# A ring of four places for read-back blocks, and two more slots between the read and the split of x, in a two-model transformer block kernel

## The chip, the cores and the metric

The kernel runs on one core of a Trainium2 chip. The metric is the device time of one execution in microseconds (us). In the profile PE is the engine that multiplies matrices, PEld its weight loads, DVE the vector engine, ACT the scalar engine, POOL the GpSimd engine, and SP the engine that here only issues DMAs.

## The reference

Two transformer blocks run one after the other on x of 256 tokens by 2048 features, all in float32. Cut to what matters here:

```python
# first block
h = rms_norm(x, norm1_g);      proj = h @ w_in              # 2048 -> 6160 columns
mix = concat([gated_linear_attention(...), dilated_attention(...)])
x = x + mix @ w_out                                         # end of stage 1
h2 = rms_norm(x, norm2_g)
x = x + (silu(h2 @ w_gate) * (h2 @ w_up)) @ w_down          # hidden 5632, end of stage 2
# second block, layer 0 (retention and convolution) and layer 1 (window attention)
x = x + even_mixer(rms_norm(x, ev_norm_w), ev_w_in, conv_w, ev_w_out)   # end of stage 3
x = x + odd_mixer(rms_norm(x, od_norm_w), od_w_in, sinks, od_w_out)
```

So a weight matrix is read once, and multiplied with 256 tokens. At three places the finished x becomes the left operand of the next weight matrix: after `w_out` (it is called X1 then), after `w_down` (X2), and after `ev_w_out` (X3).

## The kernel before, in words

**Blocks and units.** The products are cut into 96 blocks of mostly 512 output columns, and these into units of two k tiles (2 x 128 rows of the weights, 512 columns, 512 KB). Each unit is loaded into one of four places of `raw`, copied by ACT to the rounded high part `wh` (L1330) and turned by DVE into the rest `wl = raw - wh` (L1583). PE then runs three products for each k tile and each half of the tokens: `wh` by the high part of x, `wl` by the high part of x, `wh` by the low part of x (L1147 to L1149). That is 12 matmuls of 512 columns in a unit. `wh` and `wl` have three places (`NS = 3`), so ACT begins unit u once PE is through unit u - 3.

**The turned x.** PE needs x with features on partitions, in a high part `xh` (written by ACT) and a low part `xl` (written by DVE). At the end of a stage x comes out token by token in four pieces of 512 columns. Each piece is two pairs of k tiles. The last piece is turned by PE (`xturn`: L1081, then `xh<-m` and `xl<-m`). The pairs of the three pieces before are turned by way of memory: DVE transposes 32 x 32 blocks (`turn`, L1669, 2 instructions), SP writes them to the DRAM tensor `blocks` in four DMAs of 64 KB (`send`, L2154), SP reads them back in another order in one DMA of 256 KB (`fetch`, L2161), and then ACT writes `xh<-A` (2 instructions) and DVE writes `xl<-A` (4 instructions). The last two together are the step `xsent`. The same way (`msent`) is gone by the heads of the mixers.

**The norm.** `norm` is a chain of 13 small instructions on DVE (L1592 the first), which needs the sums of squares that ACT makes (`sq`, L1397, 4 instructions for each piece). Its result scales the outputs, not the operand; PE doesn't wait for it.

**The order.** A planner (`Plan`) writes one list of steps. Each engine takes its own instructions out of this list in the list's order, so the position in the list is the position in every queue. The planner goes on by slots of half a unit. A step that is due later is a generator that gives the number of slots to wait; `fetched` waits 4 slots after the send, says `fetch`, waits 4 more and says `xsent`. It also waits until the step two turns before is through, as the read-back places were two. The loads of the weights stand in SP's queue at the `cut` of unit u, for unit u + 4, and wait until `wl` of unit u is written.

**What a unit waits for.** PE's first matmul of a unit waits for `wl` of that unit (`s_lo`) and for the `xl` of its two k tiles (`s_sent` where they came by way of memory). In the first block of a stage's successor the k tiles 8 and 9 stand in the fifth unit, 10 and 11 in the sixth. In what follows "the fifth unit" and "the sixth unit" are those.

Of the kernel before, what the change touches and what calls it, by code (L numbers as in the profile page):

```python
# [33 lines left out]
class Block:  # L34


    def __init__(self, i, w, row, col, n, kts, acts, done):
        self.i, self.w, self.row, self.col, self.n, self.kts, self.acts, self.done = i, w, row, col, n, kts, acts, done
        self.units = []
# [110 lines left out]
class Plan:  # L150
# [8 lines left out]
    def __init__(self, blocks, units):  # L159
        self.order, self.said, self.there, self.norms, self.emptied = [], set(), {}, 0, set()  # L160
        self.lanes = {"first": [], "att": [], "fin": [], "post": []}
        self.pause = dict.fromkeys(self.lanes, 0)
        self.now, self.through, self.end = 0.0, {"act": 0.0, "dve": 0.0}, {}
        self.turns, self.own = [], 0
        self.blocks, self.units = blocks, units
        self.lay()

# [248 lines left out]
    def turned_and_sent(self, *p):  # L416

        if p[0] == "xsent":
            yield from self.room("dve", .8)
        self.say("turn", *p)  # L420
        self.say("send", *p)
        self.turns.append(p)
        self.spawn(self.fetched(len(self.turns) - 1, p))

    def fetched(self, n, p):
        yield 4
        while n >= 2 and self.turns[n - 2] not in self.said:
            yield 1
        self.say("fetch", *p)
        yield 4  # L430
        self.say(*p)

    def moved_by_blocks(self, key, j):
# [178 lines left out]
def program(nc, t, out):  # L612
# [7 lines left out]
    plan = Plan(blocks, units)  # L620
# [37 lines left out]
    opened = {p: n + 1 for n, p in enumerate(opens)}  # L658
# [18 lines left out]
    sents = {p: n + 1 for n, p in enumerate(q for q in plan.order if q[0] in ("xsent", "msent"))}  # L677
# [11 lines left out]
    with ctx:  # L689
        def sb(name, shape, dt=f32):  # L690
            return ctx.enter_context(nc.sbuf_tensor(name, shape, dt))

        def sem(name):
            return ctx.enter_context(nc.semaphore(name))
# [10 lines left out]
        A1 = sb("A1", [128, 6144])  # L705
        A2 = sb("A2", [128, 6144])
# [9 lines left out]
        memory = t["blocks"].rearrange("(n p) c -> n p c", n=4)  # L716
# [14 lines left out]
        s_pv, s_ob_act, s_ob_dve = sem("s_pv"), sem("s_ob_act"), sem("s_ob_dve")  # L731
        s_split = sem("s_split")
        s_turn, s_sent = sem("s_turn"), sem("s_sent")
        s_send, s_fetch = [sem("s_send0"), sem("s_send1")], [sem("s_fetch0"), sem("s_fetch1")]
        s_sq, s_nsum = sem("s_sq"), sem("s_nsum")
        s_root = sem("s_root")
        s_act_step, s_dve_step, s_pool_step = sem("s_act_step"), sem("s_dve_step"), sem("s_pool_step")
# [4 lines left out]
        s_g_sq, s_g_sum, s_g_n = sem("s_g_sq"), sem("s_g_sum"), sem("s_g_n")  # L742
# [178 lines left out]
        def raw_free(u):  # L921

            return s_lo, max((v + 1 for v in range(u) if raw_lane(v) % NR == raw_lane(u)), default=0)
# [27 lines left out]

        def turn_places(p):

            n = (sents[p] - 1) % 2
            if p[0] == "msent" and p[3] == "r":
                return PB[:, :, 256:384], A2[:, 5128:5640].rearrange("p (i n) -> p i n", i=4)
            at = {"d": A2[:, 4096:6144], "o": A2[:, 2560:4608], "X1": A2[:, 0:2048],
                  "X2": A2[:, 0:2048], "X3": A1[:, 0:2048]}[p[3] if p[0] == "msent" else p[1]]
            a, b = at[:, 512 * n:512 * n + 512], at[:, 1024 + 512 * n:1536 + 512 * n]
            return (z.rearrange("p (i n) -> p i n", i=4) for z in (a, b))  # L960

        def read_back(p, i):
# [7 lines left out]
        def sent(p):  # L970

            n = sents[p] - 1
            return s_send[n % 2], 64 * (n // 2 + 1)

        def back(p):

            n = sents[p] - 1
            return s_fetch[n % 2], 16 * (n // 2 + 1)

        def last_sent(*start):  # L980
            return [p for p in sents if p[:len(start)] == start][-1]
# [1 line left out]
        def turn_place_free(p):  # L983

            kind = p[3] if p[0] == "msent" else p[1]
            if kind == "d":
                return [(s_move, moves[("move", "qk", "k", 1, 3)])]
            if kind == "X1":
                return [(s_pv, opened[("g_o", 3)])]
            if kind == "r":  # L990
                return [(s_g_n, 4), (s_pv, opened[("apv", "d", 7)]), (s_sent, sents[p] - 1)]
            if kind == "X3":
                return [(s_pv, opened[("r_pv", 3)])]
            if kind == "o":
                return [(s_move, moves[("move", "cg", 0, 1, 3)]), (s_cmix, 4)]
            return []
# [1103 lines left out]
        def sync(e):  # L2100
            on = Once(e)

            def load(u):
                if u >= SINGLE:
                    on.wait_ge(*raw_free(u))
                weights(e, u)

            def turned_x(i):
                k0, k1 = XPARTS[i]
                e.dma_start(xT[:, k0:k1, :], t["xT"].rearrange("p (k t) -> p k t", k=KT)[:, k0:k1, :]  # L2110
                            ).then_inc(s_xt[i], 16)

            n0, n1 = COLS["n1"]
            turned_x(0)
            e.dma_start(small[:, n0:n1], t["small"][:, n0:n1]).then_inc(s_n1, 16)
            turned_x(1)
            load(2)
            turned_x(2)
            load(3)
            load(4)  # L2120
            turned_x(3)
            load(5)
            load(6)
            turned_x(4)
            load(7)
            turned_x(5)
            for p in plan.order:
                kind, a = p[0], p[1:]
                if kind == "cut" and a[0] + NR >= SINGLE and a[0] + NR < N:
                    u = a[0] + NR  # L2130
                    load(u)
                    if u == 8:
                        turned_x(6)
                    if u in (9, 11, 13, 15):
                        j = (u - 9) // 2
                        e.dma_start(x[:, :, 512 * j:512 * j + 512], t["x"].rearrange("(t p) d -> p t d", p=128)
                                    [:, :, 512 * j:512 * j + 512]).then_inc(s_x[j], 16)
                    elif u == 16:
                        e.dma_start(rel, t["rel"]).then_inc(s_rel, 16)
                        e.dma_start(oh, t["oh"]).then_inc(s_rel, 16)  # L2140
                        e.dma_start(lnn, t["lnn"]).then_inc(s_rel, 16)
                        for i in range(2):
                            e.dma_start(w2[16 * i:16 * i + 16, :], t["w2"]).then_inc(s_w2, 16)
                        e.dma_start(small[:, 0:n0], t["small"][:, 0:n0]).then_inc(s_small, 16)
                    elif u == 17:
                        e.dma_start(small[:, n1:], t["small"][:, n1:]).then_inc(s_small, 16)
                elif kind == "send":
                    n = sents[a] - 1
                    on.wait_ge(s_turn, n + 1)
                    if n >= 4:  # L2150
                        on.wait_ge(*back(plan.turns[n - 4]))
                    blocks_, _ = turn_places(a)
                    for i in range(4):
                        e.dma_start(memory[n % 4].rearrange("(b p) (i n) -> i p b n", b=4, i=4)[i],  # L2154
                                    blocks_[32 * i:32 * i + 32]).then_inc(s_send[n % 2], 16)
                elif kind == "fetch":
                    n, (_, to) = sents[a] - 1, turn_places(a)
                    on.wait_ge(*sent(a))
                    if n >= 2:
                        on.wait_ge(s_sent, n - 1)  # L2160
                    e.dma_start(to, memory[n % 4].rearrange("p (i n) -> p i n", i=4)).then_inc(s_fetch[n % 2], 16)  # L2161
                elif kind == "out":
                    j = a[0]
                    if j == 3:
                        on.wait_ge(s_added, 1)
                        e.dma_start(out[0:128, 1536:2048], x[:, 0, 1536:2048]).then_inc(s_out, 16)
                        on.wait_ge(*x_ready(4, 3))
                        e.dma_start(out[128:256, 1792:2048], x[:, 1, 1792:2048]).then_inc(s_out, 16)
                        continue
                    on.wait_ge(*x_ready(4, j))  # L2170
                    for k in range(2):
                        e.dma_start(out[128 * k:128 * k + 128, 512 * j:512 * j + 512],
                                    x[:, k, 512 * j:512 * j + 512]).then_inc(s_out, 16)
            on.wait_ge(s_out, 144)
# [84 lines left out]
```

## Time and profile before

| | |
|---|---|
| median of 3 runs | 1910.68 us (1908.93 to 1910.83) |
| the profiled execution, its own time | 1909.77 us |
| its span | 1907.7 us |
| PE busy | 1900.2 us |
| DVE busy | 1263.3 us |
| ACT busy | 1000.2 us |

PE is called busy from the start of a matmul to its modelled end, and the matmuls overlap: they follow each other every 0.23 us though one is given 0.39 us. The time that PE is not busy is what is left of the span, and with the spacing of the matmuls' starts it is what has to be looked at. The profiled execution took 2.1 us more than its span, and lies 0.9 us under the median.

### The profile page before, as it was taken

The numbers are of one execution on the slowest core, as the hardware profiler recorded it, in microseconds if no ns is written. First come the engines' busy times: TensorE is split into PE (matmuls) and PEld (weight loads), VectorE is DVE, ScalarE is ACT, GpSimd is POOL, SyncE is SP. The second block draws the span as 40 slices with busy tenths as digits, with TensorE's granted clock in tenths as the row PEclk, the third lists the DMA queues.
The fourth block names the chain that finished last, engine by engine and source line by source line (L and its number), as shares of the span: only waits on it lengthen the run. The fifth ranks groups of instructions, "written<-read, shape, count | busy, mean of one in ns | idle before, by whom it ended". The sixth has DMA issues, their size and how long they took to land.

```text
span 1907.7 us, 22767 instructions
## 1 busy us (share of the span) xinstructions
PE 1900.2 (100%) x8691; PEld 1563.0 (82%) x8691; DVE 1263.3 (66%) x1899; ACT 1000.2 (52%) x1409; POOL 14.6 (1%) x32
## 2 busy tenths in 40 slices
PE   9999999999999999999999999999999999999999
PEld 7888887888888888888888888888888888888887
DVE  6676566776667456664466767745766677688775
ACT  6777554454444344443444456554555555666653
POOL 0001000000000000000000000000000000000000
PEclk9999999999999999999999999999999999999999
DMA  9667764676666666666666676666676576555555
GB/s 317 195 199 177 205 185 129 201 230 195 196 192 194 192 193 190 196 197 192 194 192 195 216 240 191 195 194 183 188 210 194 192 253 188 163 172 174 170 160 167
DMA packets 207324, 372.18 MB, mean 195 GB/s; under 512 B 14112, under 2 KB 31824, under 8 KB 207216
## 3 DMA queue, kind: packets, MB, share of 16 engines
q1 hardware_dynamic: 205968, 367.97, 63.2%
q0 software_dynamic: 816, 2.11, 0.9%
q8 instruction: 68, 1.11, 0.2%
q10 hardware_dynamic: 432, 0.66, 0.1%
q14 instruction: 40, 0.33, 0.1%
HBM read 359.92 MB, written 10.76 MB: 194 GB/s over the span
## 4 chain that ended last, share of the span: by engine, by line
PE 98%; DMA 1%; DVE 0%; SPq 0%; ACT 0%; issue 0%; DVEq 0%; ACTq 0%
PE g L1147 31%; PE g L1149 31%; PE g L1148 31%; PE m L1216 1%; DMA A<-blocks 1%; PE m L1081 1%; PE ob L1234 0%; PE ob L1233 0%; PE ob L1232 0%; PE m L1208 0%; PE m L1206 0%; DMA A<-in_xT 0%; PE m L1300 0%; PE ob L1287 0%; PE ob L1281 0%; DVE wl L1583 0%
## 5 line engine op out<-in xcount | busy, mean ns | idle before, releaser
L1583 DVE TENSOR_TENSOR wl<-raw,wh 128x1024 fp32r<-128x1024 f32 (+1 forms) x660 | 801.6, 1217 | 547.5 <-ACT wh L1330 544.6
L1330 ACT ACTIVATE wh<-raw 128x1024 fp32r<-128x1024 f32 (+1 forms) x661 | 695.8, 1054 | 701.2 <-PE g L1149 697.1
L1147 PE MATMUL g<-wh,xh 128*128 128x512 f32 x1886 | 742.6, 394 | 1.5 <-DVE wl L1583 1.2
L1149 PE MATMUL g<-wh,xl 128*128 128x512 f32 x1886 | 734.8, 390 | 0.0
L1148 PE MATMUL g<-wl,xh 128*128 128x512 f32 x1886 | 734.1, 389 | 0.0
L1147 PEld LDWEIGHTS g<-wh,xh 128*128 128x128 f32 x1886 | 354.1, 188 | 81.5 <-issue 7.4
L1149 PEld LDWEIGHTS g<-wh,xl 128*128 128x128 f32 x1886 | 354.1, 188 | 74.3
L1148 PEld LDWEIGHTS g<-wl,xh 128*128 128x128 f32 x1886 | 354.3, 188 | 71.7
L1147 PE MATMUL g<-wh,mh 128*128 128x512 f32 x732 | 287.4, 393 | 1.0 <-DVE wl L1583 1.0
L1149 PE MATMUL g<-wh,ml 128*128 128x512 f32 x732 | 285.0, 389 | 0.0
L1148 PE MATMUL g<-wl,mh 128*128 128x512 f32 x732 | 285.0, 389 | 0.0
L1147 PEld LDWEIGHTS g<-wh,mh 128*128 128x128 f32 x732 | 137.4, 188 | 33.3 <-issue 3.9
L1149 PEld LDWEIGHTS g<-wh,ml 128*128 128x128 f32 x732 | 137.4, 188 | 28.9
L1148 PEld LDWEIGHTS g<-wl,mh 128*128 128x128 f32 x732 | 137.5, 188 | 27.7
L1711 DVE STREAM_TRANSPOSE A<-A 32x256 f32<-32x256 f32 x176 | 76.7, 436 | 2.8
L1583 DVE TENSOR_TENSOR x<-g,x 128x512 f32<-128x512 f32 (+1 forms) x73 | 46.5, 678 | 12.1 <-PE g L1149 6.8
L1327 ACT ACTIVATE A<-g,st 128x512 f32<-128x512 f32 x50 | 31.7, 684 | 30.1 <-PE g L1149 30.0
L1330 ACT ACTIVATE PT<-m 128x384 f32<-128x384 f32 x40 | 17.9, 489 | 47.6 <-PE m L1216 47.6
L1330 ACT ACTIVATE mh<-A 128x256 fp32r<-128x256 f32 (+1 forms) x56 | 27.0, 509 | 28.0 <-DVE A L1711 16.4
L1330 ACT ACTIVATE A<-TW 32x256 f32<-32x256 f32 x96 | 40.1, 418 | 1.5
L1586 DVE SCALAR_TENSOR_TENSOR xl<-A,small,xh 128x128 fp32r<-128x128 f32 (+1 forms) x88 | 27.5, 371 | 16.2 <-ACT xh L1330 16.2
L1456 ACT ACTIVATE PB<-PB,st 128x128 f32<-128x128 f32 x80 | 35.7, 451 | 1.9 <-DVE st L1592 1.8
(158 smaller groups left out, 819.6 us busy)
## 6 DMA issues: line engine op xcount, KB each, us to landing
raw<-in_ev_w_in SPq DMA_DIRECT2D x128, 512.0 KB, 3.7
raw<-in_w_in SPq DMA_DIRECT2D x92, 512.0 KB, 4.3
raw<-in_w_gate SPq DMA_DIRECT2D x88, 512.0 KB, 4.5
raw<-in_w_up SPq DMA_DIRECT2D x88, 512.0 KB, 4.0
raw<-in_w_down SPq DMA_DIRECT2D x88, 512.0 KB, 4.7
raw<-in_od_w_in SPq DMA_DIRECT2D x72, 512.0 KB, 3.8
raw<-in_w_out SPq DMA_DIRECT2D x32, 512.0 KB, 4.5
raw<-in_ev_w_out SPq DMA_DIRECT2D x32, 512.0 KB, 4.7
```

Of the source, the lines that this page charges most:

```text
L1081: last = e.transpose(dst(c), src(c), ident)
L1147: e.matmul(o, hi[:, kt, c], h, start=first, stop=False)
L1148: e.matmul(o, hi[:, kt, c], l, start=False, stop=False)
L1149: last = e.matmul(o, lo[:, kt, c], h, start=False, stop=end)
L1216: last = e.transpose(o[:, 128 * c:128 * c + 128], L[:, 128 * c:128 * c + 128], ident)
L1327: return e.activation(o, i, func, scale=scale, bias=bias)
L1330: return e.activation(o, i, AF.Copy, scale=scale)
L1456: last = e.activation(L[:, lo:hi], L[:, lo:hi], AF.Exp, bias=mx[:, h, kb:kb + 1], accum_out=sm[:, h, kb:kb + 1])
L1583: return e.tensor_tensor(o, a, b, op)
L1586: return e.scalar_tensor_tensor(out=o, in0=a, scalar=s, in1=b, op0=op0, op1=op1)
L1711: last = e.transpose(dst, src)
```

## The change

The read-back places become a ring of four for the blocks of x and of the window attention (two for the dilated heads, one for the retention heads, as before). A fetch waits for the step that used its place before, by the planner's record `before`, and no more for the one two turns back. The semaphores of the fetches become four. For blocks of x the planner waits 6 slots in place of 4 between `fetch` and `xsent`. No instruction's size changes, and none is added or taken out; some are moved.

```diff
-        self.spawn(self.fetched(len(self.turns) - 1, p))
-
-    def fetched(self, n, p):
+        group = p[1] if p[0] == "xsent" else p[3]
+        there = [q for q in self.turns if self.place[q][0] == group]
+        ring = {"d": 2, "r": 1}.get(group, 4)
+        self.place[p] = group, len(there) % ring
+        self.before[p] = there[-ring] if len(there) >= ring else None
+        self.turns.append(p)
+        self.spawn(self.fetched(p))
+
+    def fetched(self, p):
         yield 4
-        while n >= 2 and self.turns[n - 2] not in self.said:
+        while self.before[p] and self.before[p] not in self.said:
             yield 1
         self.say("fetch", *p)
-        yield 4
+        yield 6 if p[0] == "xsent" else 4
         self.say(*p)
...
-            at = {"d": A2[:, 4096:6144], "o": A2[:, 2560:4608], "X1": A2[:, 0:2048],
-                  "X2": A2[:, 0:2048], "X3": A1[:, 0:2048]}[p[3] if p[0] == "msent" else p[1]]
-            a, b = at[:, 512 * n:512 * n + 512], at[:, 1024 + 512 * n:1536 + 512 * n]
+            first, then = {"d": (A2[:, 4096:5120], A2[:, 5120:6144]), "o": (A2[:, 2560:3584], A2[:, 3584:5632]),
+                           "X1": (A2[:, 0:1024], A2[:, 4096:6144]), "X2": (A2[:, 0:1024], A2[:, 4096:6144]),
+                           "X3": (A1[:, 0:1024], A1[:, 1024:3072])}[group]
+            a, b = first[:, 512 * n:512 * n + 512], then[:, 512 * i:512 * i + 512]
...
-                return [(s_pv, opened[("g_o", 3)])]
+                return [(s_pv, opened[("g_o", 3)]), (s_g_n, 4)]
...
-                    if n >= 2:
-                        on.wait_ge(s_sent, n - 1)
-                    e.dma_start(to, memory[n % 4].rearrange("p (i n) -> p i n", i=4)).then_inc(s_fetch[n % 2], 16)
+                    if plan.before[a]:
+                        on.wait_ge(s_sent, sents[plan.before[a]])
+                    e.dma_start(to, memory[n % 4].rearrange("p (i n) -> p i n", i=4)).then_inc(s_fetch[n % 4], 16)
```

The order moves at the three passages from one x to the next, and nowhere else: 43 of the 2720 steps of the planner's list get another place. Two engine queues at two of these places follow; in them `xl<-A` is the low part of a pair that came by way of memory, `xl<-m` of a pair turned by PE, `wl<-raw,wh` the rest of a unit's weights, `x<-g,x` the addition of a finished block, `STREAM_TRANSPOSE` the turn, and the small operations on `st` the norm.

DVE before, at the passage to X1 (it is the same at X3), from the low part of k tiles 8 and 9 to the beginning of the norm:

```order
L1586 SCALAR_TENSOR_TENSOR xl<-A2,small,xh 128x128 x4
L1583 TENSOR_TENSOR wl<-raw,wh 128x1024
L1586 SCALAR_TENSOR_TENSOR xl<-m2,small,xh 128x256 x2
L1586 SCALAR_TENSOR_TENSOR xl<-A2,small,xh 128x128 x4
L1583 TENSOR_TENSOR wl<-raw,wh 128x1024 x2
L1592 TENSOR_REDUCE st<-st 128x2
L1599 TENSOR_SCALAR st<-st 128x2
```

Both `xl<-A2` stand here ahead of the norm, and two `wl` between the last of them and the norm.

DVE with the change, the same place, up to the beginning of the norm:

```order
L1593 SCALAR_TENSOR_TENSOR xl<-m1,small,xh 128x256 x2
L1590 TENSOR_TENSOR wl<-raw,wh 128x1024
L1593 SCALAR_TENSOR_TENSOR xl<-m2,small,xh 128x256 x2
L1590 TENSOR_TENSOR wl<-raw,wh 128x1024
L1593 SCALAR_TENSOR_TENSOR xl<-A2,small,xh 128x128 x4
L1590 TENSOR_TENSOR wl<-raw,wh 128x1024
L1599 TENSOR_REDUCE st<-st 128x2
```

and from the norm's beginning on:

```order
L1599 TENSOR_REDUCE st<-st 128x2
L1606 TENSOR_SCALAR st<-st 128x2
L1596 TENSOR_SCALAR st<-st 128x2
L1608 TENSOR_SCALAR st<-st 128x2
L1593 SCALAR_TENSOR_TENSOR st<-st 128x2
L1590 TENSOR_TENSOR st<-st 128x2
L1593 SCALAR_TENSOR_TENSOR st<-st 128x2 x2
L1590 TENSOR_TENSOR st<-st 128x2
L1593 SCALAR_TENSOR_TENSOR st<-st 128x2 x2
L1590 TENSOR_TENSOR st<-st 128x2
L1593 SCALAR_TENSOR_TENSOR st<-st 128x2
L1593 SCALAR_TENSOR_TENSOR xl<-A2,small,xh 128x128 x4
```

The first `xl<-A2` (k tiles 8 and 9) has gone behind the second `xl<-m` and two `wl`; the second (k tiles 10 and 11) now stands behind the whole norm.

DVE before, at the passage to X2, from the last turn of the second piece on:

```order
L1669 STREAM_TRANSPOSE A2<-x 128x2x4x32 x2
L1586 SCALAR_TENSOR_TENSOR xl<-A2,small,xh 128x128 x4
L1583 TENSOR_TENSOR wl<-raw,wh 128x1024
L1586 SCALAR_TENSOR_TENSOR xl<-A2,small,xh 128x128 x4
L1583 TENSOR_TENSOR wl<-raw,wh 128x1024 x2
L1586 SCALAR_TENSOR_TENSOR xl<-A2,small,xh 128x128 x4
L1583 TENSOR_TENSOR x<-g2,x 128x512
L1583 TENSOR_TENSOR x<-g3,x 128x512
L1583 TENSOR_TENSOR wl<-raw,wh 128x1024
L1586 SCALAR_TENSOR_TENSOR xl<-A2,small,xh 128x128 x4
```

DVE with the change, from the same turn on:

```order
L1676 STREAM_TRANSPOSE A2<-x 128x2x4x32 x2
L1590 TENSOR_TENSOR wl<-raw,wh 128x1024
L1593 SCALAR_TENSOR_TENSOR xl<-A2,small,xh 128x128 x4
L1590 TENSOR_TENSOR wl<-raw,wh 128x1024
L1593 SCALAR_TENSOR_TENSOR xl<-A2,small,xh 128x128 x4
L1590 TENSOR_TENSOR wl<-raw,wh 128x1024
L1590 TENSOR_TENSOR x<-g2,x 128x512
L1590 TENSOR_TENSOR x<-g3,x 128x512
L1590 TENSOR_TENSOR wl<-raw,wh 128x1024 x2
L1676 STREAM_TRANSPOSE A2<-x 128x2x4x32 x2
L1593 SCALAR_TENSOR_TENSOR xl<-A2,small,xh 128x128 x4
```

The third `xl<-A2` of this piece of the queue stood ahead of the addition and of the `wl` that follows it. Now it stands behind both, and behind one more `wl` and the turn of the third piece, which has itself moved up by two units. The norm at X2 stands behind the last `xl` both before and now.

## Rows read from the trace of the kernel before

**Rows 1.** Page, part 1: busy us, share of the span, instructions.

```profile
PE 1900.2 (100%) x8691; PEld 1563.0 (82%) x8691; DVE 1263.3 (66%) x1899; ACT 1000.2 (52%) x1409; POOL 14.6 (1%) x32
```

**Rows 2.** Windows, PE alone: length, busy us, granted clock, DMA share, GB/s.

```profile
0.00:50.00 50.00, 47.01 (x190) 1.00 0.90 310
...
1080.00:1120.00 40.00, 38.95 (x172) 1.00 0.81 251
...
1580.00:1907.70 327.70, 324.27 (x1650) 1.00 0.56 171
```

**Rows 3.** Waits of PE: who, for whom, us in total, times, longest.

```profile
PE g L1147 <- DVE wl L1583: 2.3, 2, 1.2
```

**Rows 4.** Timeline, PE near 1107: start, us, line, out<-in [idle before <-releaser].

```profile
1106.20 0.39 PE L1149 MATMUL g<-wh,ml 128*128 128x512 f32 x1
1107.63 0.50 PE L1147 MATMUL g<-wh,mh 128*128 128x512 f32 x1 [1.05 <-DVE wl L1583]
1107.97 0.40 PE L1148 MATMUL g<-wl,mh 128*128 128x512 f32 x1
```

**Rows 5.** Timeline, PE at the passage to X2.

```profile
1118.64 0.39 PE L1147 MATMUL g<-wh,xh 128*128 128x512 f32 x1
```

**Rows 6.** Timeline, DVE near 1107.

```profile
1104.11 1.14 DVE L1586 SCALAR_TENSOR_TENSOR xl<-A,small,xh 128x128 fp32r<-128x128 f32 x4 [2.52 <-ACT xh L1330]
1105.17 1.28 DVE L1583 TENSOR_TENSOR x<-g,x 128x512 f32<-128x512 f32 x2
1106.37 1.21 DVE L1583 TENSOR_TENSOR wl<-raw,wh 128x1024 fp32r<-128x1024 f32 x1
```

**Rows 7.** Chain that ended last, in order of time: start, us, what.

```profile
1096.71 6.36 DMA A<-blocks
```

**Rows 8.** DMA issues: what, count, KB each, median us to landing.

```profile
A<-blocks SPq DMA_DIRECT2D x33, 256.0 KB, 4.7
```

**Rows 9.** Timeline, ACT at the passage to X1.

```profile
401.30 0.84 ACT L1330 ACTIVATE xh<-m,small 128x256 fp32r<-128x256 f32 x2 [2.17 <-PE m L1081]
...
406.14 0.91 ACT L1330 ACTIVATE xh<-A,small 128x256 fp32r<-128x256 f32 x2
406.94 1.06 ACT L1330 ACTIVATE wh<-raw 128x1024 fp32r<-128x1024 f32 x1
407.89 0.63 ACT L1397 ACTIVATE TE<-x 128x512 f32<-128x512 f32 x1
...
409.28 2.00 ACT L1330 ACTIVATE wh<-raw 128x1024 fp32r<-128x1024 f32 x2
```

**Rows 10.** Timeline, PE at the passage to X1.

```profile
397.81 0.50 PE L1147 MATMUL g<-wh,xh 128*128 128x512 f32 x1
...
400.67 0.60 PE L1081 MATMUL m<-small,x 128*128 128x128 f32 x4
...
403.88 0.60 PE L1081 MATMUL m<-small,x 128*128 128x128 f32 x4
...
409.98 0.50 PE L1147 MATMUL g<-wh,xh 128*128 128x512 f32 x1
...
412.83 0.39 PE L1147 MATMUL g<-wh,xh 128*128 128x512 f32 x1
```

**Rows 11.** Timeline, DVE at the passage to X1.

```profile
407.65 1.14 DVE L1586 SCALAR_TENSOR_TENSOR xl<-A,small,xh 128x128 fp32r<-128x128 f32 x4
...
411.50 0.15 DVE L1592 TENSOR_REDUCE st<-st 128x2 f32<-128x8 f32 x1
...
413.95 2.35 DVE L1583 TENSOR_TENSOR wl<-raw,wh 128x1024 fp32r<-128x1024 f32 x2
```

**Rows 12.** Timeline, PE at the passage to X3.

```profile
1565.68 0.39 PE L1147 MATMUL g<-wh,xh 128*128 128x512 f32 x1
...
1580.25 0.39 PE L1147 MATMUL g<-wh,xh 128*128 128x512 f32 x1
```

**Rows 13.** Waits of SP's queue: fetch line, for whom, us in total, times, longest.

```profile
SPq L2161 <- DMA blocks<-A: 3.1, 6, 1.2
...
SPq L2161 <- DMA blocks<-PB: 0.8, 1, 0.8
```

More of the change, by code:

```diff
@@ L163, in __init__ @@
         self.now, self.through, self.end = 0.0, {"act": 0.0, "dve": 0.0}, {}
-        self.turns, self.own = [], 0
+        self.turns, self.own, self.place, self.before = [], 0, {}, {}
         self.blocks, self.units = blocks, units
@@ L733, in program @@
         s_turn, s_sent = sem("s_turn"), sem("s_sent")
-        s_send, s_fetch = [sem("s_send0"), sem("s_send1")], [sem("s_fetch0"), sem("s_fetch1")]
+        s_send, s_fetch = [sem("s_send0"), sem("s_send1")], [sem(f"s_fetch{i}") for i in range(4)]
         s_sq, s_nsum = sem("s_sq"), sem("s_nsum")
@@ L952, in turn_places @@
         def turn_places(p):
-            n = (sents[p] - 1) % 2
-            if p[0] == "msent" and p[3] == "r":
+            n, (group, i) = (sents[p] - 1) % 2, plan.place[p]
+            if group == "r":
                 return PB[:, :, 256:384], A2[:, 5128:5640].rearrange("p (i n) -> p i n", i=4)
-            at = {"d": A2[:, 4096:6144], "o": A2[:, 2560:4608], "X1": A2[:, 0:2048],
-                  "X2": A2[:, 0:2048], "X3": A1[:, 0:2048]}[p[3] if p[0] == "msent" else p[1]]
-            a, b = at[:, 512 * n:512 * n + 512], at[:, 1024 + 512 * n:1536 + 512 * n]
+            first, then = {"d": (A2[:, 4096:5120], A2[:, 5120:6144]), "o": (A2[:, 2560:3584], A2[:, 3584:5632]),
+                           "X1": (A2[:, 0:1024], A2[:, 4096:6144]), "X2": (A2[:, 0:1024], A2[:, 4096:6144]),
+                           "X3": (A1[:, 0:1024], A1[:, 1024:3072])}[group]
+            a, b = first[:, 512 * n:512 * n + 512], then[:, 512 * i:512 * i + 512]
             return (z.rearrange("p (i n) -> p i n", i=4) for z in (a, b))
@@ L977, in back @@
             n = sents[p] - 1
-            return s_fetch[n % 2], 16 * (n // 2 + 1)
+            return s_fetch[n % 4], 16 * (n // 4 + 1)
         def last_sent(*start):
```

## The prediction, made before the changed kernel ran

> **What bounds the kernel now.** I read the engines' busy times first. PE is busy for 1900.2 of 1907.7 us [rows 1], so there are 7.5 us at most that any change of order can win. The windows show where they lie: 3.0 us in the first 50 us, 1.05 us between 1080 and 1120, and 3.4 us in the stretch that holds the end [rows 2]. Those three make up all 7.5. The change touches neither the beginning nor the end, so only the 1.05 us lie near it. The granted clock is 1.00 in every window, which is the upper level, 2.4 GHz.
>
> The waits of PE agree: it waited for `wl` twice, the longer time 1.2 us (at the start of the kernel), the other time 1.05 us [rows 3, 4]. The second is the passage to X2. The timeline of PE gives its whole price. Four units (1107.63 to 1118.64) take 11.01 us [rows 4, 5]; less 0.11 for a slow start that is explained next, a unit is 2.72 us and a matmul 0.227. From 1106.20 to 1107.63 are 1.43 us, which is 1.20 more than one matmul; then the next start comes 0.34 us later and not 0.227, which is 0.11 more. So this wait costs 1.31 us, and a new wait of any length will cost its length and 0.11.
>
> Why it waits is in DVE's timeline: `xl<-A` sat 2.52 us idle for `xh`, then the addition ran, then the `wl` for which PE waited, from 1106.37 to 1107.58 [rows 6]. Behind the `xh` is a read from memory that took 6.36 us [rows 7], where the median of 33 is 4.7 [rows 8]. A late block of X2, which PE wants only 20 us later, holds up a unit's weights that PE wants now, because both stand in one queue.
>
> **The change part by part.** Its sizes are the same, so there is no work to add up, only waits.
>
> *Passage to X2.* The `xl` that came too late now stands behind the addition and that `wl`. PE would have begun the unit at 1106.43, so ACT may begin its `wh` two units before, at 1101.0. With 1.06 for `wh` [rows 9], 1.28 for the addition and 1.21 for `wl` [rows 6], `wl` is done by about 1103.8 even if ACT and DVE wait for each other: 2.6 us ahead of need. The wait goes: -1.3 us. What is late next there is the norm, which stands between the `wl` of the sixth and the seventh unit. The first unit would begin at 1118.64 - 1.31 = 1117.33. PE's turns of the last piece cost 0.47 each: five units with both take 14.57 us at X3 [rows 12], less 13.60. The second turn stands in the middle of the third unit: 1117.33 + 5.44 + 0.47 + 1.36 = 1124.6. ACT begins 0.63 after it (401.30 less 400.67, [rows 9, 10]) and needs 0.84 for `xh`, 1.39 for the squares (409.28 less 407.89), 1.06 for `wh` [rows 9]: 1128.5. DVE needs 1.21 for `wl`, 2.45 for the norm (411.50 to 413.95, [rows 11]), 1.21 for the next `wl`: 1133.4. The seventh unit begins at 1117.33 + 16.32 + 0.94 = 1134.6. It holds, with 1.2 us to spare.
>
> *Passages to X1 and X3.* Here PE had hardly a wait before. At X3 from the first to the sixth unit it took 14.57 us [rows 12]; at X1 15.02 us [rows 10]. So at X1 PE lost 0.45 us in small delays that the busy time hides, and at X3 none. With the change two steps of the sixth unit's supply trade places: the low part of k tiles 10 and 11 now stands behind the norm. I follow the chain at X1. PE's second turn is at 403.88 [rows 10]; ACT starts at 404.51, `xh` of the turn to 405.35, `wh` of the fifth unit to 406.41, squares to 407.80, `xh` of k tiles 8 and 9 (0.91) to 408.71 [rows 9]. DVE follows with `xl` (1.14, [rows 11]) to 409.85, `wl` of the sixth unit (1.21) to 411.06, the norm to 413.51, and `xl` of k tiles 10 and 11 to 414.65. These are sums of whole durations; in the timelines the next instruction of an engine begins about 0.1 us before the one ahead has ended (406.14 + 0.91 is 407.05, the next starts at 406.94), and with seven such seams it is 414.0. I take 414.4. PE would be ready for the sixth unit at 397.81 + 14.57 = 412.38. So it waits 2.0 us, and pays 0.11 for the restart. Against before (412.83) the sixth unit at X1 begins 1.6 later: +1.7 with the restart. At X3 the whole chain stands in the same order and there were no small delays to win: +2.1 us. Each of the two terms may be 0.4 smaller (414.0) or 0.3 larger (414.65), and it is nothing at all if the norm is out of the way, which is a rival below.
>
> The other side of the fifth unit: `xl` of k tiles 8 and 9 is done at 409.5 to 409.85, and PE is ready for it at 412.38 - 2.72 = 409.66. That is even; up to 0.2 us may be lost, which the later wait would then contain, as the chain on ACT and DVE isn't longer for it.
>
> *The reads.* They have more time now. At X1 the read of k tiles 8 and 9 is issued behind a load that waits for the second `wl` of the new block. ACT may begin that unit when PE is one unit short of the block, at 395.1, and 1.06 and 1.21 with an `xl` of 1.14 between make 398.5. With the 6.36 of the slow read [rows 7] it is there by 404.9, where ACT comes for it at 407.8. The one of 10 and 11 goes out one unit later, 401, and is there by 407.4 where 408.7 is asked. The gain of two slots is real, but nothing on PE's path waited for the reads at X1 and X3, so nothing comes of it.
>
> *The ring, the four semaphores, the added wait on `s_g_n`.* In the waits of SP's queue the fetches stood behind their own sends, 7 times for 3.9 us, and never for a place [rows 13]; the mixers' heads keep their order. The added wait is for a step that ended long before on the same engine. I cost these at nothing, from -0.1 to +0.1 us, since PE had no idle time outside the windows named.
>
> **The sum.** -1.3 + 1.7 + 2.1 = +2.5 us. The profiled execution took 1909.77, so it would be 1912.3. The median of the runs shown is 1910.68; the middle of the four executions is 1910.2, from which I start: 1912.7 us. That is 0.13% slower, under the 0.2% (3.8 us) that a measurement of this kernel can tell from no change.
>
> **The clock.** The granted clock stayed at 1.00 through the 1.43 us between two matmuls at 1107 [rows 2, 4]. The two new waits are about 2.2 us long, longer than any in the rows, and nothing in this trace shows what the clock does after such a one. The Trainium skill, "TensorE: Matmul & The Clock Gate", section "Why this matters for your kernels", says that pauses between bursts of matmuls can drop the engine to its slower level. By that rule there would be a rival of its own; the trace so far is against it, since its waits left the clock alone. Worked out from the rows as a mechanism: at half the clock a unit of 2.72 us takes 5.44; if I take two units at the lower level after each new wait it is 4 x 2.72 = 10.9 us more, 1923.6.
>
> **The rivals.**
> - *Only the gain.* DVE gets to the norm earlier than I think, or PE is later, and the norm's 2.45 us fit in ahead of the sixth unit. Then -1.3 and the 0.45 of X1 are won: -1.75, which is 1908.5. For it: PE was never stopped there before. Against it: in my chain there is no idle time of DVE between the low part of k tiles 8 and 9 and the norm, and it would have to be shorter by 2 us. Chance 0.10.
> - *Slower by over 0.2%: the norm is in the way at X2 also.* There 1.2 us are to spare. If DVE comes 1.2 us late to the norm, as it does when a read of X2 takes 7 us and more or the additions wait, the seventh unit waits, and each microsecond more costs one. With the same 2.1 us of wait as at X3 it is 1.7 + 2.1 + 2.1 - 1.3 = +4.6, so 1914.8; it decides from 1.3 us of wait at X2 on, which brings the sum to 3.8. For it: the reads varied from 4.7 to 6.36. Against it: between a read and its split there are now three units where there were two. Chance 0.09.
> - *The clock*, 1923.6. Chance 0.03.
> - *The change doesn't do what it says*: the wait at X2 stays (a read that is late still stands in ACT's queue), and the two new ones come: +3.8 to +3.9, 1914.0. Chance 0.04.
>
> **How the numbers follow.** My forecast, both new waits and the old one gone, has 0.74. Its own range is from +1.6 to +3.1 by the bounds of the two new terms, and the base is uncertain by 1 us either way (1908.93 to 1910.83): 1910.8 to 1914.3. The range of 1909.2 to 1915.6 takes in part of the gain alone at its lower end and the wait at X2 at its upper end. Faster by over 0.2% would need 3.8 us where only 1.75 are to be had near the change: 0.02. Slower by over 0.2%: 0.03 for the clock, 0.06 from the rival at X2, 0.02 from the last one, 0.03 from the forecast where a measured base or a term lies at its upper end: 0.14. The rest, 0.84, is no change that can be told.
>
> **What would show it.** In the waits of PE the 1.05 us near 1107 are gone. New are two waits of PE for DVE of about 1.9 us each, near 412.4 and 1580 less 1.3 plus 1.7, each ended by an `xl<-A` that starts where the norm's last instruction ends. PE's busy time stays, and the span less the busy time rises from 7.5 to about 10. The read's landing no longer ends an idle time of ACT at X2. If PE starts the sixth unit at X1 before 413, the chain on ACT and DVE is wrong; if an idle time of PE stands ahead of the seventh unit at X2, the rival is right; a clock under 1.00 in a window behind 414 would show the other.

## The result, and the profile after

The changed kernel takes 1912.26 us in the median of 20 runs (1911.18 to 1913.83), the kernel before 1909.49 (1908.38 to 1912.28). The ratio is 1.0014, 95% interval 1.0007 to 1.0020: slower by 2.7 us, which is clear of zero and within the 0.2% that was called no change. Forecast were 1912.7 us, +2.5.

The page's first part for the changed kernel, and below it the windows of PE (length, busy us, granted clock, DMA share, GB/s), to be set beside [rows 1, 2]:

```profile
PE 1900.4 (100%) x8691; PEld 1562.8 (82%) x8691; DVE 1263.2 (66%) x1899; ACT 999.0 (52%) x1409; POOL 14.4 (1%) x32
```

```profile
0.00:50.00 50.00, 47.52 (x193) 1.00 0.91 313
...
380.00:420.00 40.00, 38.36 (x172) 1.00 0.78 235
...
1080.00:1140.00 60.00, 60.00 (x270) 1.00 0.81 250
...
1540.00:1590.00 50.00, 48.33 (x216) 1.00 0.79 243
```

The work is the same to 0.2 us. The span went from 1907.7 to 1909.5, and all of it is idle time of PE: 7.5 us before, 9.2 now. The 1.05 us at X2 are gone (60.00 of 60.00), 1.64 us at X1 and 1.67 at X3 are new, and the first 50 us lost 0.5 less this time, at a place that the change doesn't touch. The clock stayed at 1.00.

The waits of PE name the releaser, and PE's timeline at X1 the place (start, us, line, out<-in [idle before <-releaser]); they answer to [rows 3, 10]:

```profile
PE g L1154 <- DVE xl L1593: 4.2, 4, 1.7
```

```profile
397.26 0.39 PE L1154 MATMUL g<-wh,xh 128*128 128x512 f32 x1
...
409.18 0.47 PE L1154 MATMUL g<-wh,xh 128*128 128x512 f32 x1
...
411.79 0.39 PE L1156 MATMUL g<-wh,xl 128*128 128x512 f32 x1
413.82 0.47 PE L1154 MATMUL g<-wh,xh 128*128 128x512 f32 x1 [1.64 <-DVE xl L1593]
```

From the first to the sixth unit are 413.82 - 397.26 = 16.56 us, where 15.02 were before. At X3 the same stretch goes from 1565.42 to 1581.98, again 16.56, where 14.57 were [rows 12]. DVE at X1, beside [rows 11]:

```profile
407.89 1.14 DVE L1593 SCALAR_TENSOR_TENSOR xl<-A,small,xh 128x128 fp32r<-128x128 f32 x4 [1.01 <-ACT xh L1337]
408.95 1.22 DVE L1590 TENSOR_TENSOR wl<-raw,wh 128x1024 fp32r<-128x1024 f32 x1
410.08 0.15 DVE L1599 TENSOR_REDUCE st<-st 128x2 f32<-128x8 f32 x1
...
412.45 0.16 DVE L1593 SCALAR_TENSOR_TENSOR st<-st 128x2 f32<-128x2 f32 x1
412.54 1.14 DVE L1593 SCALAR_TENSOR_TENSOR xl<-A,small,xh 128x128 fp32r<-128x128 f32 x4
```

DVE stands still nowhere for more than 0.05 us from the low part of k tiles 8 and 9 (407.89) to the end of that of 10 and 11 (413.68), and PE starts 0.14 us after that. The norm lies in the middle of it, from 410.08 to 412.54.

The waits of ACT for the reads from memory (who, for whom, us, times, longest), first of the kernel before and then of the changed one, show what the two more slots did to the reads:

```profile
ACT xh L1330 <- DMA A<-blocks: 20.2, 14, 3.4
```

```profile
ACT xh L1337 <- DMA A<-blocks: 0.2, 1, 0.2
```

### The profile page after: what moved, and what is told of

It is laid out like the page before. It is cut to its first block, busy times and chain, and to the rows that moved or that the text cites. A ratio compares the mean times of both kernels' runs of the same rounds, so it can differ in the third digit from the quotient of the medians.

```text
span 1909.5 us, 22749 instructions
## 1 busy us (share of the span) xinstructions
PE 1900.4 (100%) x8691; PEld 1562.8 (82%) x8691; DVE 1263.2 (66%) x1899; ACT 999.0 (52%) x1409; POOL 14.4 (1%) x32
## 4 chain that ended last, share of the span: by engine, by line
PE 98%; DVE 1%; DMA 1%; ACT 0%; issue 0%; SPq 0%; DVEq 0%; ACTq 0%
PE g L1154 31%; PE g L1156 31%; PE g L1155 31%; PE m L1223 1%; DMA raw<-in_w_in 1%; PE m L1088 1%; PE ob L1241 0%; PE ob L1240 0%; PE ob L1239 0%; PE m L1215 0%; PE m L1213 0%; DVE xl L1593 0%; PE m L1307 0%; PE ob L1294 0%; PE ob L1288 0%; DVE wl L1590 0%
## 5 line engine op out<-in xcount | busy, mean ns | idle before, releaser
L1590 DVE TENSOR_TENSOR ml<-A,mh 128x256 fp32r<-128x256 f32 (+1 forms) x56 | 28.9, 538 | 7.6 <-ACT mh L1337 7.6
```

Of the source, the lines that this page charges most:

```text
L1590: return e.tensor_tensor(o, a, b, op)
```

## The experiments

**E1: the slots without the ring.** The kernel before with

```diff
-        yield 4
+        yield 6 if p[0] == "xsent" else 4
         self.say(*p)
```

> The kernel before with six slots in place of four between the read and the split of x, and the old two places (no ring). Theory (the order alone does it; the ring does nothing): all engines' queues are as in the changed kernel, so PE waits 1.65 us at X1 and at X3 ahead of the sixth unit, none near 1107, and the time is the changed kernel's, +2.5 us against before (ratio 1.0013). Rival (the ring takes part, or its places and semaphores cost): without the ring a fetch waits for its place, the reads land later, and the time or the waits differ from the changed kernel's by 1 us or more.

Measured: 1912.0 us, ratio to before 1.0008 (0.9999 to 1.0016), span 1909.6 beside 1909.5 of the changed kernel. Windows of PE:

```profile
380.00:420.00 40.00, 38.34 (x173) 1.00 0.76 236
...
1080.00:1140.00 60.00, 60.00 (x270) 1.00 0.82 251
...
1540.00:1590.00 50.00, 48.34 (x217) 1.00 0.81 242
```

The same three windows as in the changed kernel, to 0.02 us. For PE the whole effect is in the slots, and none of it in the ring. The ratio alone wouldn't have said so, as its interval touches no change; the profile does. The condition of the rival did come, but not its cost: at X2 two reads stood in SP's queue until the `xl` that used their place was written, 1.3 and 1.1 us (SP's waits for `xl`, in no profile of a kernel with the ring and not in that of before). ACT then waited 2.1 us in all for reads of x, 4 times, where it was 0.2 us in the changed kernel. PE lost nothing by it.

**E6: the ring without the slots.** The changed kernel with `yield 4` at that place, so that every queue has the order of before.

> The changed kernel with four slots again: the ring, its semaphores and the wait for a place's last user stay, and all queues are as in the kernel before. Theory: the ring alone changes nothing, ratio 1.0000 within 0.1%; in its profile ACT waits about 20 us for the reads of x as before, and PE waits 1 to 2 us in all at the passages because of them. Rival (the ring lets the reads go out earlier): ACT's waits for the reads of x fall under 10 us, and the time is 1 us or more under that of before.

Measured: 1910.83 us, ratio 1.0001 (0.9992 to 1.0010). Its waits of ACT and its wait of PE near 1108:

```profile
ACT xh L1337 <- DMA A<-blocks: 21.1, 12, 3.8
```

```profile
1108.00 0.50 PE L1154 MATMUL g<-wh,mh 128*128 128x512 f32 x1 [1.36 <-DVE wl L1590]
```

Both are much as before (20.2 and 1.05 us). With four slots no read waited for a place, with two places [rows 13] or with four; with six slots and two places some do (E1), and the ring takes that wait away.

**E2: six slots at X2 alone.** The changed kernel with

```diff
-        yield 6 if p[0] == "xsent" else 4
+        yield 6 if p[:2] == ("xsent", "X2") else 4
```

> The changed kernel with six slots at X2 alone and four at X1 and X3. Theory: the wait at 1107 goes (1.31 us with the restart) and the two waits at X1 and X3 are not there: -1.3 us against before (ratio 0.9993); PE's busy time stands 6.4 us under the span. Rival (the gain at X2 isn't real, what is saved there comes back later in the same passage): the same time as before.

Measured: 1909.03 us, ratio 0.9991 (0.9982 to 1.0000), -1.7 us. The interval touches no change, so that the gain at X2 isn't given back rests on the profile and on the spans below. In its profile PE waited none at X2, but 0.22 us at X1 and twice at X3, where the order was that of before. PE and ACT at X3:

```profile
1563.08 0.50 PE L1154 MATMUL g<-wh,mh 128*128 128x512 f32 x1 [0.84 <-DVE wl L1590]
...
1569.41 0.66 PE L1088 MATMUL m<-small,x 128*128 128x128 f32 x4 [0.48 <-DVE x L1590]
```

```profile
1559.74 0.91 ACT L1337 ACTIVATE xh<-A,small 128x256 fp32r<-128x256 f32 x2 [4.50 <-DMA A<-blocks]
```

This is the same thing as at X2 in the kernel before: ACT stood 4.50 us for a read, and the units behind it came late. With four slots the loss at X2 stands in all three profiles that have them there (1.05, 1.36 in E6, 1.06 in E7). At X3 one of four shows a loss, this one; at X1 one shows 0.22 us. So the prediction's "nothing comes of it" for the reads at X1 and X3 was true of one execution and not of all. The spans of all executions give an estimate of the mean. In one series of runs their median was 1908.1 us for the kernel before, 1906.8 for this one, 1906.3 for E3 and 1905.8 for E4 (both below, with later splits at X1 and X3 too). That is 1.3 us for X2, as forecast, and some 0.5 to 1.0 us that four slots cost at X1 and X3 together.

**E3: the norm two slots later.** The changed kernel with

```diff
                 if j == 3:
-                    yield 2
+                    yield 4
                     say("norm", stage)
```

> The changed kernel with the norm said two slots later, so that it stands behind the second xl of the pairs that came by way of memory and behind the wl of the seventh unit. Theory (the norm's 2.45 us on DVE are what PE waits for at X1 and X3): both waits of 1.65 us go, that at 1107 stays away, and the small delays of X1 (0.45 us) too: -1.7 us against before, -4.2 against the changed kernel. Rival (the splits of x are late in themselves, because they are done two slots later): the waits of PE at the sixth unit stay over 0.5 us each, and the time is +0 to +2 us against before.

Measured: 1908.35 us, ratio to before 0.9990 (0.9981 to 0.9999). The windows of PE, and DVE at X1:

```profile
380.00:420.00 40.00, 40.00 (x181) 1.00 0.80 241
...
1080.00:1140.00 60.00, 60.00 (x271) 1.00 0.83 253
...
1540.00:1590.00 50.00, 50.00 (x225) 1.00 0.82 248
```

```profile
409.30 1.22 DVE L1590 TENSOR_TENSOR wl<-raw,wh 128x1024 fp32r<-128x1024 f32 x1
410.44 1.13 DVE L1593 SCALAR_TENSOR_TENSOR xl<-A,small,xh 128x128 fp32r<-128x128 f32 x4
411.49 1.22 DVE L1590 TENSOR_TENSOR wl<-raw,wh 128x1024 fp32r<-128x1024 f32 x1
```

The same splits at the same late place, and no wait: `xl` of k tiles 10 and 11 is done at 411.57. It follows its `wl` at once, the norm comes after the next. This rules out that the splits or the reads were too late in themselves. Expected were -1.7 us, measured are -1.9.

**E7: the late norm alone**, the same edit in the kernel before.

> The kernel before (two places, four slots) with the norm said two slots later, nothing else. Theory: where the splits stand ahead of the norm the norm is in nobody's way, so this wins nothing: ratio 1.0000 within 0.1%, with PE's wait near 1107. Rival (the late norm is itself what won in the run of the changed kernel with the norm late): about -2 us (ratio 0.999).

Measured: 1910.08 us, ratio 1.0000 (0.9991 to 1.0009), and the wait of 1.06 us at 1107.57 as ever. Moving the norm wins only where the splits have moved behind it.

**E4: five slots.** The changed kernel with `yield 5`. At X1 and X3 the split of k tiles 10 and 11 gets ahead of the norm again, where it is at X2 anyway; the norm isn't touched.

> The changed kernel with five slots in place of six. The low part of k tiles 10 and 11 then stands ahead of the wl of the sixth unit and of the norm, at all three passages. Theory: no wait at X1 and X3, none at 1107: -1.7 us against before (ratio 0.9991). Rival (every slot more between read and split costs at X1 and X3, so that half of it costs half): about +0.6 us.

Measured: 1908.15 us, ratio 0.9988 (0.9980 to 0.9997), span 1905.9. PE was never idle in the windows of the three passages (40.00 of 40.00, 60.00 of 60.00, 50.00 of 50.00 us). DVE at X1, from the split of k tiles 10 and 11 to the beginning of the norm:

```profile
408.49 1.14 DVE L1593 SCALAR_TENSOR_TENSOR xl<-A,small,xh 128x128 fp32r<-128x128 f32 x4 [1.01 <-ACT xh L1337]
409.55 1.22 DVE L1590 TENSOR_TENSOR wl<-raw,wh 128x1024 fp32r<-128x1024 f32 x1
410.68 0.15 DVE L1599 TENSOR_REDUCE st<-st 128x2 f32<-128x8 f32 x1
```

Not the number of slots costs, but the step that the split falls behind: with one slot less the loss is not halved but gone.

**E5: the norm twice as long.** The changed kernel with 12 more instructions of two columns ahead of each norm but the first:

```diff
+                    if a[0]:
+                        v, y, q = rv_[:, 2:4], ry_[:, 2:4], rq_[:, 2:4]
+                        on.wait_ge(s_nsum, a[0] + 1)
+                        on.wait_ge(*steps.mark(e.tensor_scalar(v, nsum, 1.0 / D, 1e-6, ALU.mult, ALU.add)))
...
+                        for i in range(3):
+                            on.wait_ge(*steps.mark(stt(q, v, -0.5, y, ALU.mult, ALU.mult)))
+                            on.wait_ge(*steps.mark(tt(q, q, y, ALU.mult)))
+                            on.wait_ge(*steps.mark(stt(y, q, 1.5, y, ALU.add, ALU.mult)))
                     root(rr, nsum, 2, D, (s_nsum, a[0] + 1), free)
```

> The changed kernel with 12 more small instructions on DVE ahead of each of the norms at X1, X2 and X3 (the same chain as the norm's root on two spare columns; its result isn't used), about 2.4 us more for each. Theory (the norm's length on DVE is the wait): PE's waits at the sixth unit grow from 1.65 to about 4.05 us at X1 and at X3; at X2, where the changed kernel's trace has the wl of the seventh unit ready at 1134.3 and PE there at 1135.7, a new wait of 1.1 us appears. Together +6.0 us against the changed kernel, +8.8 against before (ratio 1.0046). Rival (PE waits at the sixth unit for the moved splits or reads themselves): no more than 1 us longer. A further question: whether the granted clock falls behind a pause of 4.1 us; if it does, a window behind the pause shows less than 1.00 and the time is 10 us and more longer.

Measured: 1922.82 us in 5 runs, ratio 1.0061 (1.0048 to 1.0073), +11.7 us against before, where 8.8 were expected without the clock. PE's timeline, first at X2 and X3, then at X1, and windows behind X1:

```profile
1142.33 0.50 PE L1154 MATMUL g<-wh,xh 128*128 128x512 f32 x1 [0.91 <-DVE wl L1590]
...
1591.11 0.76 PE L1154 MATMUL g<-wh,xh 128*128 128x512 f32 x1 [4.02 <-DVE xl L1593]
...
1596.34 0.39 PE L1154 MATMUL g<-wh,xh 128*128 128x512 f32 x1
```

```profile
412.55 0.39 PE L1156 MATMUL g<-wh,xl 128*128 128x512 f32 x1
416.96 0.77 PE L1154 MATMUL g<-wh,xh 128*128 128x512 f32 x1 [4.02 <-DVE xl L1593]
417.52 0.63 PE L1155 MATMUL g<-wl,xh 128*128 128x512 f32 x1
417.95 0.63 PE L1156 MATMUL g<-wh,xl 128*128 128x512 f32 x1
...
422.17 0.40 PE L1154 MATMUL g<-wh,xh 128*128 128x512 f32 x1
```

```profile
410.00:415.00 5.00, 2.94 (x13) 1.00 0.52 166
415.00:417.00 2.00, 0.04 (x1) 0.57 0.00 0
417.00:420.00 3.00, 3.00 (x7) 0.50 0.20 45
420.00:422.00 2.00, 2.00 (x6) 0.50 1.04 376
422.00:424.00 2.00, 2.00 (x9) 0.98 0.23 89
```

The waits grew by what the chain grew: 1.64 to 4.02 and 1.67 to 4.02 (2.4 expected), and at X2, where 1.35 us were to spare in the changed kernel (the `wl` done at 1134.34, PE there at 1135.69), 0.91 appeared (1.1 expected). These and the restart at X2 make 5.8 us, where 6.0 against the changed kernel were expected. The rest is the clock. Behind both pauses of 4.02 us it is at 0.50, the lower level (at X3 from 1593 to 1596), and the 12 matmuls of the next unit take 5.21 us and 5.23 (422.17 - 416.96, 1596.34 - 1591.11) in place of 2.72: 2.4 to 2.5 more each. So the question on the clock is answered with yes, at some 5 us for both and not the "10 us and more" that were written. The first 50 us lost 0.85 us more than in the changed kernel's profile, which closes the difference of the two profiled spans (1921.1 less 1909.5, 11.6) to 0.1.

**E8: the slots and the late norm, without the ring**, both edits in the kernel before.

> The kernel before with the old two places, six slots for x and the norm two slots later: the candidate without the ring. Theory (the ring does nothing): the same as the changed kernel with the norm late, -2.1 us against before (ratio 0.999), no wait of PE at any of the three passages. Rival (the ring is needed with six slots): some reads wait for a place, ACT waits over 3 us for reads of x, and the time is over that of the changed kernel with the norm late by 1 us or more.

Measured: 1907.91 us, ratio 0.9986 (0.9977 to 0.9995), -2.7 us. PE had no idle time in the windows of the three passages; ACT waited 1.6 us for reads of x. Two reads of X2 waited for their place, 2.2 us in all, as in E1, and it cost PE nothing. E3, E4 and E8 are faster than before with intervals that leave out no change, by 1.9 to 2.7 us; the profiled spans are 1906.0, 1905.9 and 1905.7 beside 1907.7 before and 1909.5 with the change, and the theory gives -1.75 against before (1.3 at X2, 0.45 at X1). Their intervals overlap, and which of the three is best is not told apart.

## Why the prediction was right

- *The passage to X2 (-1.3).* Right. The wait went, and the norm there stayed out of the way with 1.35 us to spare (1.2 worked out). E2 shows the gain by itself, E5 the margin, by using it up.
- *X1 (+1.7).* 16.56 less 15.02 and 0.09 for the restart make 1.63.
- *X3 (+2.1).* 16.56 less 14.57 and 0.09 make 2.08. The chain of durations was to end 16.6 us behind the first unit (414.4 - 397.81) and ended at 16.56. Part of that is luck: the `xl` was done 16.42 us behind the first unit, 0.17 sooner than the chain had it, and PE began 0.14 us after it, which the chain left out.
- *The pause.* I gave the wait as 2.0 us, counted from where an undelayed PE would begin the sixth unit. Counted so it is 1.99 (413.82 less 397.26 + 14.57), but not all of it is this pause. From the last start to the next are 2.03 us (411.79 to 413.82), of which 0.227 are the matmul's own spacing: 1.80 are lost in the pause, and 0.19 went in small delays ahead of it, nearly all in and just before the fifth unit. At X3 it is 1.82 and 0.17. That is the "up to 0.2 us" which the prediction saw at the fifth unit, and said that the later wait would contain. PE's idle column says 1.64 and 1.67, since it counts only from the modelled end of the matmul; so the "about 1.9" of the list of signs was too long for that column, and the idle time rose to 9.2 us and not to 10.
- *The ring at nothing.* Right in cost, by E1 and E6. The reason given, that no fetch ever waits for a place, is read from the kernel with four slots. With six slots and no ring two fetches do (E1, E8), and PE doesn't feel it.
- *The reads "more time, and nothing comes of it".* Right in the two profiles, too narrow as a rule: E2 shows that with four slots X3 can wait too. By the spans the six slots save some 0.5 to 1.0 us of lateness at X1 and X3 in the mean (an estimate, see E2), in which the 0.45 us of small delays at X1 are contained; a sum from one execution can't see the rest.
- *The rival of the clock* was rightly kept small for pauses of 2 us: three profiles with such pauses (the changed kernel, E1 and, with 1.36 us, E6) stayed at 1.00. E5 shows that it is real at twice the length. Its price was put at two units at the lower level; it was one.

The time itself came nearer than its parts: the base was put at 1910.2 and measured 1909.49, the change at 2.5 and measured 2.7, and the two errors partly cancel. The terms make +2.4 by the timelines. The measured +2.7 agrees within its interval (1.3 to 3.8 us); the profiled executions differ by 1.8, as the beginning of the kernel was 0.5 us shorter after.

## What to carry to other kernels

Where PE is busy nearly all the time, as here, a change of order is priced by the waits at the passages: follow each moved instruction in its queue and ask what now stands ahead of it, above all a chain of tiny dependent instructions, which costs its latency and not its work (here 2.45 us for 13 instructions of two columns). A wait for a late transfer is best moved back in the queue, but only up to the next long step; here one slot decided between -0.1% and +0.1%. Compare the windows of the profile first when a ratio's interval touches 1.

## What the runs showed of the hardware

Behind a pause of 2.0 us between the starts of two matmuls the granted clock stayed at 1.00; behind one of 4.4 us (412.55 to 416.96) it was at 0.50 and came back at the end of 12 matmuls, which took 5.2 us. So a pause that lost 4.2 us between the starts (4.0 in the idle column) cost 6.7 with the slow unit behind it. The Trainium skill, "TensorE: Matmul & The Clock Gate", section "Why this matters for your kernels", says that long pauses between bursts take the engine to the slower level; the trace of E5 agrees, and gives the price. Behind the waits of 0.9 to 1.7 us the successor of the first matmul came about 0.1 us late (0.31 to 0.34 us in place of 0.227). A read of 256 KB took 4.7 us in the median of 33 and 6.36 behind the wait at 1107, beside the stream of the weights. The same queue order at X3 left PE idle there for 0 us in the profiles of before and E6 and for 1.3 us in that of E2.
